# An MLP loop turned by half a period: first half of the tokens up and down, then the other

## What is computed

```python
x = layer_norm(ALPHA * x + mixer(x, ...), ln1_g[i], ln1_b[i])
x = layer_norm(ALPHA * x + jnp.square(jax.nn.relu(x @ w_up[i])) @ w_down[i], ln2_g[i], ln2_b[i])
# D_MODEL = 1024, D_FF = 4096, ALPHA = (2 * DEPTH) ** 0.25, DEPTH = 2
```

## Time and profile before

| what | value |
|---|---|
| runs | 1216.31, 1217.06, 1217.19 us |
| profiled execution, span | 1216.0 us |
| TensorE matmul busy | 1133.9 us, 93% |
| VectorE busy | 717.3 us, 59% |
| ScalarE busy | 519.7 us, 43% |
| GpSimd busy | 246.4 us, 20% |
| mean granted TensorE clock | 0.962 |

### The profile page before, as it was taken

How to read it: one execution, slowest core, us unless ns; L and a number is a source line. 1 busy time by engine, 2 the same in 40 slices (tenths; PEclk the granted TensorE clock), 3 DMA queues, 4 the chain that set the end, 5 groups by cost and what they waited for, 6 DMA issues and landing times.

```text
span 1216.0 us, 23224 instructions
## 1 busy us (share of the span) xinstructions
PE 1133.9 (93%) x8783; PEld 1106.2 (91%) x8783; DVE 717.3 (59%) x1283; ACT 519.7 (43%) x1016; POOL 246.4 (20%) x277
## 2 busy tenths in 40 slices
PE   7898798899999999999799889989999999999993
PEld 6788798899999999999799558979999999999992
DVE  6887879744545445445961881596444444444457
ACT  5778745622412323225553892363423324224132
POOL 4344335300000000001460681261000000000025
PEclk9899899899999999999899897989999999999996
DMA  7222124222222222222120120032223223232102
GB/s 248 79 78 82 58 70 152 96 88 86 86 86 86 86 86 86 86 86 87 53 85 26 53 70 18 2 117 75 86 86 102 71 89 101 76 97 76 62 1 74
DMA packets 51462, 98.32 MB, mean 81 GB/s; under 512 B 4448, under 2 KB 20256, under 8 KB 51392
## 3 DMA queue, kind: packets, MB, share of 16 engines
q1 hardware_dynamic: 50720, 94.81, 24.9%
q0 software_dynamic: 400, 2.21, 0.5%
q10 hardware_dynamic: 288, 0.59, 0.1%
HBM read 95.06 MB, written 3.56 MB: 81 GB/s over the span
## 4 chain that ended last, share of the span: by engine, by line
PE 76%; DVE 13%; ACT 4%; POOL 3%; issue 3%; DMA 1%; SPq 1%; POOLq 0%; DVEq 0%; ACTq 0%
PE bank L1297 23%; PE bank L1298 23%; PE bank L1299 23%; DVE w_lo L774 2%; PE bank L1358 1%; PE bank L1359 1%; PE bank L1360 1%; DVE xc_odd L914 1%; DVE acc L999 1%; DVE rstd L1001 1%; POOL w_lo L1274 1%; DVE acc L1005 1%; DVE x_lo L994 1%; DMA acc<-xs_t 1%; PE bank L1491 1%
## 5 line engine op out<-in xcount | busy, mean ns | idle before, releaser
L1297 PE MATMUL bank<-x_hi,w_hi 128*128 128x288 f32 (+1 forms) x1360 | 397.1, 292 | 12.0 <-DVE w_lo L774 12.0
L1298 PE MATMUL bank<-x_lo,w_hi 128*128 128x288 f32 (+1 forms) x1360 | 395.5, 291 | 0.0
L1299 PE MATMUL bank<-x_hi,w_lo 128*128 128x288 f32 (+1 forms) x1360 | 393.4, 289 | 0.0
L1297 PE MATMUL bank<-m_hi,w_hi 128*128 128x288 f32 (+1 forms) x1120 | 323.8, 289 | 0.0
L1298 PE MATMUL bank<-m_lo,w_hi 128*128 128x288 f32 (+1 forms) x1120 | 322.8, 288 | 0.0
L1299 PE MATMUL bank<-m_hi,w_lo 128*128 128x288 f32 (+1 forms) x1120 | 321.1, 287 | 0.0
L467 ACT ACTIVATE w_hi<-stage 128x1024 fp32r<-128x1024 f32 x170 | 173.4, 1048 | 272.8 <-PE bank L1299 268.1
L1297 PEld LDWEIGHTS bank<-x_hi,w_hi 128*128 128x128 f32 x1360 | 259.3, 191 | 13.5 <-DVE w_lo L774 12.9
L1299 PEld LDWEIGHTS bank<-x_hi,w_lo 128*128 128x128 f32 x1360 | 259.9, 191 | 0.0
L1298 PEld LDWEIGHTS bank<-x_lo,w_hi 128*128 128x128 f32 x1360 | 259.5, 191 | 0.0
L774 DVE TENSOR_TENSOR w_lo<-stage,w_hi 128x1024 fp32r<-128x1024 f32 x162 | 204.3, 1268 | 44.2 <-ACT w_hi L467 44.1
(11 more groups left out here) (182 smaller groups left out, 1300.8 us busy)
## 6 DMA issues: line engine op xcount, KB each, us to landing
stage<-w_up SPq DMA_DIRECT2D x64, 512.0 KB, 3.7
stage<-w_down SPq DMA_DIRECT2D x64, 512.0 KB, 3.3
stage<-w_qkv SPq DMA_DIRECT2D x10, 512.0 KB, 3.6
stage<-w_x SPq DMA_DIRECT2D x8, 512.0 KB, 4.7
stage<-w_y SPq DMA_DIRECT2D x8, 512.0 KB, 4.5
stage<-w_out SPq DMA_DIRECT2D x8, 512.0 KB, 5.2
stage<-w_o SPq DMA_DIRECT2D x8, 512.0 KB, 3.7
y_t<-acc SPq DMA_DIRECT2D x8, 144.0 KB, 1.9
```

The source lines that it names most:

```text
L1297: mm(out, wh, xh, start=(k == 0), stop=False)
L1298: mm(out, wh, xl, start=False, stop=False)
L1299: ins = mm(out, wl, xh, start=False, stop=(k == last))
```

## The change

The loop's contents stay the same, their order is turned. After the first up units, a pass is: down of chunk c for h1, up of chunk c+1 for h0, down of chunk c+1 for h0, up of chunk c+1 for h1. The first four down units of a half run with k outermost, so that each k waits only for its own `m_lo` tile (`down` on TensorE). The splits of the four up slabs of the next chunk now stand beside the 8 down units of h1, those of the four down slabs beside the 4 up units of h0, one split ahead of each.

At the start of an MLP TensorE takes two up units of h0, the `norm_sums` of h1, two more up units, the 8 down units of h0, and then the group of four up units of h1. ScalarE and VectorE split all four down slabs before the norm of h1 is begun, take up units 0 and 1 before it, and VectorE takes up unit 2 after the subtraction of the mean and up unit 3 after the reciprocal. VectorE adds the down units of h0 only after the whole norm of h1.

At the end of an MLP the norm of h0 stands beside two up units and all 8 down units of h1. VectorE adds the h1 tiles after the norm of h0 and, in layer 0, after the four splits of the first q/k/v slabs. Then q/k/v takes four units of h0, the `norm_sums` of h1, four more units of h0 (the next group of slabs), and only then h1.

```diff
 def plan_mlp(l):
+    plan(("up", l), "AA")
     plan(("ln", 2 * l, 1), "AV")
-    plan(("up", l), "A" * 8)
-    plan(("loop", l), ("V" * 16 + "A" * 8) * (CHUNKS - 1))
-    plan_tiles("down", 2 * l + 1)
+    plan(("up_rest", l), "AA")
+    plan(("first", l), "V" * 8 + "A" * 4)
+    plan(("loop", l), ("V" * 8 + "A" * 4 + "V" * 8 + "A" * 4) * (CHUNKS - 2))
+    plan(("last", l), "V" * 8 + "A" * 4 + "V" * 8 + "AA")
+    plan(("ln", 2 * l + 1, 0), "AV")
+    plan(("last_up", l), "AA")
+    plan(("last_down", l), "V" * 8)
...
 # ScalarE, mlp(l)
+split(range(j0 + 4, j0 + 8))
+up(l, 0)
+up(l, 1)
 norm_stats(2 * l, 1)
+up(l, 2)
+up(l, 3)
+norm_apply(2 * l, 1)
 for q in range(4, 8):
     up(l, q)
+with act.Fori(0, CHUNKS - 2) as i:
+    split(range(j0 + 8, j0 + 12), i, 8, 24, up_unit(l, 0, 1, 3) + 1)
+    for q in range(4):
+        split([j0 + 12 + q], i, 8, 24, down_unit(l, 0, 1, 7) + 1)
+        up(l, q, 1, i)
+    for q in range(4, 8):
+        up(l, q, 1, i)
...
 # VectorE, mlp(l)
 split(range(j0 + 4, j0 + 6))
+up(l, 0)
+split(range(j0 + 6, j0 + 8))
+up(l, 1)
 norm_stats(2 * l, 1)
+norm_apply(2 * l, 1, after_centre=lambda: up(l, 2), after_root=lambda: up(l, 3))
+for m in range(KT):
+    dve.wait_ge(s_res, 32 * l + m + 1)
+    accumulate(l, 0, 0, m)
+for q in range(4, 8):
+    up(l, q)
+with dve.Fori(0, CHUNKS - 2) as i:
+    for m in range(KT):
+        if m < 4:
+            split([j0 + 8 + m], i, 8)
+        accumulate(l, 0, 1, m, i)
+    for q in range(4):
+        split([j0 + 12 + q], i, 8)
+        up(l, q, 1, i)
+    for m in range(KT):
+        accumulate(l, 1, 0, m, i)
+    for q in range(4, 8):
+        up(l, q, 1, i)
...
+for m in range(KT):
+    add_tile("down", L, 0, m)
+up(l, 4, CHUNKS - 1)
+up(l, 5, CHUNKS - 1)
+norm_stats(L, 0)
+norm_apply(L, 0, after_centre=lambda: up(l, 6, CHUNKS - 1), after_root=lambda: up(l, 7, CHUNKS - 1))
+if l == 0:
+    split(next_slabs(("qkv", 0)))
+for m in range(KT):
+    add_tile("down", L, 1, m)
...
 # TensorE
+def down(l, c, h, w0, i=0):
+    for m in range(4):
+        loop_bank(down_unit(l, c, h, m), i)
+    for k in range(4):
+        pe.wait_ge(s_hlo, i * 8 + (t0 + k + 1))
+        for m in range(4):
...
+group_by_k(range(u0, u0 + 2), 0, ...)
+norm_sums(2 * l, 1)
+up(l, 0, 0, w0, ts=(2, 3))
+pe.wait_ge(s_wlo, j0 + 8)
+down(l, 0, 0, w0)
+group_by_k(range(u1, u1 + 4), 1, ...)
+with pe.Fori(0, CHUNKS - 2) as i:
+    down(l, 0, 1, w0, i)
+    pe.wait_ge(s_wlo, i * 8 + (j0 + 12))
+    up(l, 1, 0, w0, i)
+    pe.wait_ge(s_wlo, i * 8 + (j0 + 16))
+    down(l, 1, 0, w0, i)
+    up(l, 1, 1, w0, i)
```

More of the change, by code:

```diff
@@ L243, in build @@
         plan_mlp(0)
+        plan(("qkv", 0, 0), "AAAA")
         plan(("ln", 1, 1), "AV")
-        for g in range(3):
-            for h in (0, 1):
-                plan(("qkv", g, h), "AAAA" if g < 2 else "AA")
+        for g, h in ((1, 0), (0, 1), (1, 1), (2, 0), (2, 1)):
+            plan(("qkv", g, h), "AAAA" if g < 2 else "AA")
         mark["attention"] = len(reader)
@@ L1050, in mlp @@
             def mlp(l):
                 j0 = job_at[("mlp", l)][0]
+                j7 = j0 + 8 * (CHUNKS - 1)
+                L = 2 * l + 1
                 split(range(j0 + 4, j0 + 6))
+                up(l, 0)
+                split(range(j0 + 6, j0 + 8))
+                up(l, 1)
                 norm_stats(2 * l, 1)
[L1055 to L1060, removed]
@@ new lines, in mlp @@
+                for m in range(KT):
+                    if m < 4:
+                        split([j7 + m])
+                    accumulate(l, CHUNKS - 2, 1, m)
+                for q in range(4):
+                    split([j7 + 4 + q])
+                    up(l, q, CHUNKS - 1)
+                for m in range(KT):
+                    add_tile("down", L, 0, m)
+                up(l, 4, CHUNKS - 1)
+                up(l, 5, CHUNKS - 1)
+                norm_stats(L, 0)
+                norm_apply(L, 0, after_centre=lambda: up(l, 6, CHUNKS - 1), after_root=lambda: up(l, 7, CHUNKS - 1))
@@ L1083, in _ @@
             qj = job_at[("qkv", 1)][0]
-            split(range(qj, qj + 2))
+            split(range(qj, qj + 4))
             norm_stats(1, 1)
-            norm_apply(1, 1, lambda t: split(range(qj + 1 + t, qj + 2 + t)) if t in (1, 2) else None)
+            norm_apply(1, 1)
             split(range(qj + 4, qj + 6))
@@ new lines, in up, with loop_bank @@
+            def up(l, c, h, w0, i=0, ts=range(4)):
+                for t in ts:
+                    n0 = up_unit(l, c, h, t)
+                    loop_bank(n0, i)
+                    product(n0, HALF[h][1], quad_pieces(w0, t, h))
+            def loop_bank(n, i):
+                prev = n - BANKS
+                who = reader[prev]
+                if who == "A":
+                    pe.wait_ge(s_evA, i * 8 + read_by(prev + 1, "A"))
+                else:
+                    pe.wait_ge(s_evV, i * 16 + read_by(prev + 1, "V"))
@@ L1457, in scores @@
+                down(l, CHUNKS - 1, 0, w0)
+                up(l, CHUNKS - 1, 1, w0, ts=(0, 1))
+                norm_sums(2 * l + 1, 0)
+                up(l, CHUNKS - 1, 1, w0, ts=(2, 3))
+                down(l, CHUNKS - 1, 1, w0)
             def scores(T):
@@ L1536, in qkv @@
                     product(n0 + t, HALF[h][1], quad_pieces(w0, t, h))
-            for g in range(2):
-                for h in range(2):
-                    qkv(g, h)
+            qkv(0, 0)
+            norm_sums(1, 1)
+            for g, h in ((1, 0), (0, 1), (1, 1)):
+                qkv(g, h)
             ident = V("ident", 0, 128)
```

154 lines of the change are left out of this document (80 added, 74 removed).

## The result

After the change the kernel takes 1236.6 us (median of 4 runs, 1235.7 to 1237.3), against 1217.0 us before on the same chip: a ratio of 1.0165, interval 1.015 to 1.0179. The profiled execution has a span of 1233.8 us and a mean clock of 0.971. One of the ten executions of experiment 4 took 1376.2 us at a clock of 0.747 and is left out of the comparisons.

The account below looks back on a forecast made before the run. TensorE was taken to bound the kernel, 93% busy, idle at four norm stages losing 36.5 us. Terms 6.4 + 13.4 + 10.5 - 4.9 - 5.2 = +20.2 us gave 1237.3 us; own range 1230 to 1245, 8-in-10 range 1223 to 1249.

Parts of the forecast that it names:

- The loop: MLP passes: TensorE waits for the last down slab's w_lo, 0.75 us a pass, 14 passes, +10.5 us.
- A: Start of MLP 0, norm of h1: late down slab costs 7.5 us, stage 21.9 against 8.5, +13.4 us.
- B: End of MLP 0 into q/k/v: waits for q/k/v splits 4.8 us, stage 8.2 against 13.1, -4.9 us.
- D: End of MLP 1 to last output: last sums wait 2.2 instead of 6.9 us, tail 0.5 less, -5.2 us.
- the bank wait: MLP starts: h1 up group waits for h0 down tiles' banks, added only after the norm, 4.2 us each.
- C: Start of MLP 1, norm of h1 not hidden: stage 14.4 against 8.0, +6.4 us.
- The loop holds: Rival, MLP passes: no stall per pass, 1226.8 us; chance 0.22.
- The loop loses more: Rival, MLP passes: 1.5 us lost per pass, 1247.8 us; chance 0.15.
- the second group's slabs: q/k/v after MLP 0: h0's eight units cover the norm of h1 except 1.5 us for these slabs.
- The norms are hidden: Rival, MLP start: down h0 covers the norm of h1; 1186 us, or 1196 with the loop's stall; chance 0.08.
- The clock: Rival, MLP passes: short waits lose TensorE's clock, 2 us each, 28 in all, 1265 us; chance 0.03.
- The exclusion of VectorE and GpSimd: Norms: the two engines exclude each other, 1.4 us once or twice in each norm.

Follow-up runs that it names:

- experiment 4: Changed kernel with the old MLP start and GpSimd's old entry order put back, turned passes kept, first pass written out: 1216.4 us, ratio 0.9998 to the kernel before.
- experiment 9: Changed kernel with TensorE's wait for the four down slabs moved behind its bank waits and first m_lo wait: 1229.6 us, ratio 1.0109 to the kernel before.
- experiment 1: Changed kernel with every down slab in the passes split one place earlier on ScalarE and VectorE: 1221.4 us, ratio 1.0039 to the kernel before.
- experiment 3: Changed kernel with GpSimd's five cache and state transfers issued after the residuals of h1: 1228.1 us, ratio 1.0092 to the kernel before.
- experiment 11: Changed kernel with earlier down-slab splits, down tiles added inside the norm of h1, and later cache transfers together: 1204.2 us, ratio 0.9915 to the kernel before.
- experiment 2: Changed kernel with VectorE adding h0 down tiles 0 to 3 inside the norm of h1, not after it: 1224.6 us, ratio 1.0064 to the kernel before.
- experiment 8: Kernel before with only the change's q/k/v order, first block read out before the norm of the second half: 1208.5 us against 1216.05, ratio 0.9937.
- experiment 5: Changed kernel with the old MLP start put back, turned passes kept, and down slabs split one place earlier: 1202.6 us, ratio 0.9889 to the kernel before.

## Why the prediction came out right

The time forecast, 1237.3 us, is 0.7 from the measured median. That closeness is luck. The loop cost 4.6 us more than forecast (15.1 for 10.5), A, B and D together some 4 us less, and the errors cancel. What the forecast had right is the mechanism: a stall on the last down slab in each pass, the late slab in A, the bank wait in A and C, shorter waits in B and D.

- **The loop: right mechanism, too small.** The step "From the end of a VectorE write to the next matmul is some 0.14 us, and the restart some 0.1: 0.75 us a pass" was mis-sized: 1.15 us for each of the 12 passes written as a loop. The forecast put the lateness of the slab at 0.49 us, and 0.49 us it is. What stands behind it is 0.50 instead of 0.14, since TensorE first goes through five more waits; experiment 9 shows it by moving them. The last passes, with 0.6 us each, come near the forecast. Experiment 1 shows that the whole term hangs on this one slab. The rival "The loop holds" is refuted. The 1.15 us lie midway between the 0.75 of the forecast and the 1.5 of "The loop loses more". The bound of 1.5 had named waits for banks and k-order that add to the slab's, and they do, though none of them has to wait for anything.
- **A: +12.2 for +13.4.** The wait for the slab is 8.65 us for 7.5 predicted, and its cause is the one named, transfers beside GpSimd's (experiment 3). It gave some of it back at k = 2: 0.9 us where 3.2 were counted, since VectorE had caught up in the longer wait. The bank wait is 3.79 for 4.2.
- **C: +6.3 for +6.4.** The waits are 1.6, 0.4, 2.95, 1.15 and 3.8 us for 2.3, 0.8, 3.2, 1.4 and 4.2 predicted, and then half the clock, which costs 2.5 us. The waits are some 2 us less than forecast; the low clock and, by difference, the restart behind each wait, for which the sum had nothing, make up for it. And the 6.3 is that of one execution in which the clock fell at the bank wait; with the clock falling at k = 3 the same code took 1.9 to 2.5 us less (experiment 11). The bank wait was tested by itself (experiment 2). As predicted, the norm of h1 is not hidden.
- **B: -6.8 for -4.9.** One wait of 3.8 us (4.8 forecast) in place of two; the 1.5 us counted for the second group's slabs didn't come. The gain does not need the turned end, which the forecast named first: the kernel before gains 7.5 us with the q/k/v order alone (experiment 8).
- **D: one wait of 1.0 us** for the 2.2 forecast, in place of 6.8, the tail 0.6 us shorter as forecast.
- **The price of the entry** (19.0 us, experiment 4), **of the loop** (15.2, experiment 1) and **the gain at B and D** (14.1, experiment 5) give +20.1 us against 19.6 measured, and the forecast had 19.8, 10.5 and 10.1. The 15.2 of the loop holds 2.5 us of stage C (experiment 1), which the price of the entry counts too, so that the three fit within 0.5 is partly chance.
- **The rivals.** "The norms are hidden" needed the norm of h1 to start by the time of its sums; in C its statistics start at 823.5, 8.9 us after its sums, and the clean loop beside it would not have helped. Three mends and a clean loop bring 1204.2 us (experiment 11), so the 1186 us of that rival are out of reach for this entry. "The clock" is out: the pass has a granted clock of 1.00 with the wait in it. The waits of 3.8 us do lose it, and so did one of 1.1 us that came 1.8 us after one of 2.9 (experiment 2). What the rival had wrong is only that the short waits of the loop, one in 49 us, are enough. The Trainium skill ("TensorE: Matmul & The Clock Gate", part 1) says that the clock is low by default and that activity releases it; the trace agrees, at 0.50 behind the idle time of 3.8 us and 1.00 where there was none (the two windows of the group in C).
- **The exclusion of VectorE and GpSimd**, for which 1.4 us were counted in each norm, was not tested by itself, but the traces bear it out. In C of the changed kernel two steps of VectorE are long beside GpSimd's subtraction:

```profile
822.08 1.47 DVE L1083 TENSOR_TENSOR m_lo<-h_sq,m_hi 128x256 fp32r<-128x256 f32 x1
823.47 1.67 DVE L1007 TENSOR_TENSOR msq<-mean 128x288 f32<-128x288 f32 x1
...
821.67 3.15 POOL L1281 TENSOR_TENSOR acc<-acc,mean 128x576 f32<-128x576 f32 x2
```

Together they are 2.2 us over the 0.43 and 0.46 that they take elsewhere. In experiment 9 the subtraction ends 0.8 us before L1007, and L1007 takes 0.46 us.

## What to carry to other kernels

When an order is turned, ask for each preparation in it which shorter stretch is its cover now: the four splits had 24 us and got 11, and one place in a list decided on 15 us. In a loop, put the wait that ends last at the end of a row of waits, next to its reader. Where banks go round robin, which reader frees a bank decides more than how much work lies between: moving two entries of the plan took 4.4 us off a wait (1.6 came back at the next tile), and eight units of cover took off none. And run the parts of a mixed change alone: here one part of three was worth 14 us and the two others cost 34. And look in the traces at the stages that an edit left alone: here one of them moved by 2 us.

## What was unexpected in the hardware

- Waits that are already satisfied cost time when they stand behind one that is just released: five of them 0.45 us in a loop (experiment 9), where the same five in a pass that is written out cost nothing that shows (the matmul comes 0.05 us after the slab instead of 0.50, experiment 9; a gap of 0.58 us instead of 1.20, experiment 4). What differs is that the loop's wait values come from a register; that this is the cause was only argued.
- The length of a wait does not settle whether TensorE's clock falls behind it. A gap of 1.1 us in each pass of 49.4 us leaves the granted clock at 1.00, and so does a wait of 2.3 us in experiment 8. In stage C of experiments 1, 2, 3 and 9 a wait of 0.8 to 1.1 us is followed by 0.50; it ends 2.9 us after the end of another, of 1.8 to 2.95 us. The changed kernel has the same pair there (2.95, then 1.15 us) and keeps 1.00.
- The attention stretch, untouched by all the kernels here, takes 61.05 to 62.74 us from one profiled execution to the next. Span differences under 2 us between single profiles are no evidence, and medians of runs are better. With stage C as above, 2.5 us can come from a place that nobody touched.
